# Expert result rows split by the place that makes them: the first half read and added during the last place, and two layer-1 weights queued straight behind the experts'

## The reference, cut to what matters

```python
_, ik = lax.top_k(pe, TOP_K)                      # TOP_K = 2 of 8 in the best of 4 groups
wk = wk / jnp.sum(wk, -1, keepdims=True)
gate = (gmask[:, :, None] * pg_sel[:, None, None] * w_grp[:, None, :]).reshape(-1, N_EXPERTS)
hh = jax.nn.silu(h1) * h3 * gate[:, :, None].astype(t.dtype)
return jnp.einsum('tef,efd->td', hh, p['w2'])     # then x = x + g2 * (this)
```

## Time and profile before

| | |
|---|---|
| median of 3 runs | 978.43 us (975.48 to 981.66) |
| profiled execution: time, span | 978.13 us, 976.3 us |
| mean granted TensorE clock | 0.976 of full speed |
| busy: PE, DVE, ACT, POOL | 896.2, 409.5, 239.9, 120.2 us |
| DMA: bytes, mean rate | 318.85 MB, 327 GB/s |
| places 0 to 31 of layer 0 | about 238 to 468 us |
| seam, to the first projection of tile 0 | 468 to 489 us |
| last matmul to end of layer 1 | 953.1 to 976.3 us |

### The profile page before, as it was taken

One profiled execution on the slowest core, in us unless ns is written; L12 is line 12 of the kernel. 1 busy time (PEld: TensorE's weight loads), 2 busy tenths in 40 slices (PEclk: granted clock), 3 DMA queues, 4 the chain that ended last, 5 costly groups with the idle time before them and its releaser, 6 DMA issues.

```text
span 976.3 us, 14476 instructions
## 1 busy us (share of the span) xinstructions
PE 896.2 (92%) x5479; PEld 503.0 (52%) x5479; DVE 409.5 (42%) x1193; ACT 239.9 (25%) x605; POOL 120.2 (12%) x131
## 2 busy tenths in 40 slices
PE   6999989999999999888999988999989999998880
PEld 3346447556555565455366554554655555645540
DVE  2112476346522442211364576662764225222114
ACT  4020243112111111111354455442211111111111
POOL 1000000100222221211100000001002222212110
PEclk9999999999999999999999999998999999999996
DMA  9999799739999999998870039507599999999975
GB/s 373 397 406 417 292 419 419 247 142 370 364 416 418 402 417 416 418 419 328 330 254 7 1 116 351 234 1 237 212 419 415 417 418 409 417 417 418 412 297 202
DMA packets 62133, 318.85 MB, mean 327 GB/s; under 512 B 12662, under 2 KB 14198, under 8 KB 32104
## 3 DMA queue, kind: packets, MB, share of 16 engines
q1 hardware_dynamic: 46864, 287.51, 72.7%
q0 software_dynamic: 13328, 25.02, 7.4%
q10 hardware_dynamic: 1872, 5.39, 1.5%
HBM read 312.72 MB, written 26.49 MB: 347 GB/s over the span
## 4 chain that ended last, share of the span: by engine, by line
PE 66%; DMA 19%; DVE 9%; issue 2%; ACT 2%; SPq 1%; ACTq 0%; DVEq 0%; POOLq 0%
PE psum L943 15%; DMA ring<-in_l_w 15%; PE psum L956 9%; PE psum L1185 6%; PE psum L1308 3%; PE psum L892 3%; PE psum L879 3%; PE psum L1317 2%; PE psum L923 2%; DMA ring<-in_l_w_ada 2%; PE psum L790 2%; PE psum L1436 2%; PE psum L726 2%; PE psum L1349 2%; PE psum L1411 1%
## 5 line engine op out<-in xcount | busy, mean ns | idle before, releaser
L943 PE MATMUL psum<-ring,scratch 128*64 128x256 f32 x1744 | 210.5, 393 | 22.1 <-DMA ring<-in_l_w 21.1
L943 PEld LDWEIGHTS psum<-ring,scratch 128*64 128x64 f32 x1744 | 135.8, 141 | 81.4 <-issue 32.0
L2350 DVE TENSOR_TENSOR scratch<-scratch,psum 64x256 f32<-64x256 f32 x64 | 27.1, 424 | 286.1 <-ACT scratch L1604 278.9
L956 PE MATMUL psum<-ring,scratch 128*64 128x512 f32 x464 | 112.1, 603 | 1.9 <-ACT scratch L1652 1.0
L2826 POOL DMA_INDIRECT expert_rows<-scratch,slot_rows x64 | 63.5, 992 | 337.5 <-ACT scratch L1618 332.9
L1604 ACT ACTIVATE scratch<-psum 64x256 f32<-64x256 f32 x64 | 24.0, 375 | 255.9 <-PE psum L943 255.9
L1618 ACT COPY scratch<-psum 128x512 f32<-128x512 f32 x64 | 37.5, 585 | 132.1 <-PE psum L956 129.9
L1185 PE MATMUL psum<-ring,scratch 128*128 128x512 f32 (+1 forms) x168 | 63.6, 533 | 0.0
L956 PEld LDWEIGHTS psum<-ring,scratch 128*64 128x64 f32 x464 | 29.3, 136 | 41.5 <-issue 37.3
L1185 PEld LDWEIGHTS psum<-ring,scratch 128*128 128x128 f32 x168 | 31.1, 191 | 29.7 <-issue 28.7
L2332 DVE COPY scratch<-psum 128x512 f32<-128x512 f32 x64 | 41.4, 687 | 7.8 <-PE psum L905 6.9
(11 more groups left out here) (393 smaller groups left out, 1242.3 us busy)
## 6 DMA issues: line engine op xcount, KB each, us to landing
ring<-in_l_w SPq DMA_DIRECT2D x108, 1024.0 KB
ring<-in_l_w_rows SPq DMA_DIRECT2D x56, 1024.0 KB
ring<-in_l_w_ada SPq DMA_DIRECT2D x39, 1024.0 KB, 4.9
ring<-in_ada_first SPq DMA_DIRECT2D x8, 1024.0 KB
ring<-in_l_w_o SPq DMA_DIRECT2D x8, 1024.0 KB
ring<-in_l_w_in SPq DMA_DIRECT2D x4, 1024.0 KB
gate_rows<-gate_rows_hbm POOLq DMA_DIRECT2D x8, 512.0 KB, 7.6
scale_shift<-gate_rows_hbm POOLq DMA_DIRECT2D x8, 512.0 KB, 9.9
```

The source lines that it names most:

```text
L943: last = nc.tensor.matmul(ps[64 * n:64 * n + 64, 2 + par, 0:DE], mine[:, k, :], part(w, k * DE, DE), start=k == 0, stop=k == KD - 1)
L956: last = nc.tensor.matmul(ps[64 * n:64 * n + 64, 5 + par, :], hhT[:, par, k, :], part(w2, k * D + n * 512, 512), start=k == 0, stop=k == 1)
```

## The change

The last expert's rows all go to the second half of the table, so that the first half is complete one place earlier. A token whose first pick is expert 31 has its two picks' rows and gates exchanged (`turned`, `turned_base`, `moved`, `kept`: small DVE operations in the routing). Expert 31 is no longer a candidate for a second turn. For place 31, `down_step(30)` and `take_out(30)` come ahead of the place's own up-projections and silu. SP loads each tile's first rows once places 0 to 30 are stored, and the second rows once place 31 is. DVE adds each half with two operations (gate and g2 in one, then the state); ACT's `scale_pair` is gone. At the seam one `w_in` load and both `w_ukv` loads stand directly behind the experts' weights on SP, and the second stretch of filler on PE has 3 products where it had 8.

The diff, cut to its core:

```diff
@@ tiles of the rows
         def pair(t, k):
-            return view(W, 6144 + (2 * t + k) * D, D) if t < 2 else view(AB, (2 + k) * D, D)
+            if k == 0:
+                return view(W, t * D, D)
+            return view(W, 7168 + 2 * t * D, D) if t < 2 else view(AB, 3 * D, D)
@@ SP
-            def rows_stored(l):
+            def first_rows_stored(l):
                 sp.wait_ge(S[f"ov_out{l}"], 16)
-                for buf in range(2):
-                    sp.wait_ge(S[f"y_out{buf}"], 16 * (l + 1) * PAIRS)
+                sp.wait_ge(S["y_out0"], 16 * (l + 1) * PAIRS)
+                sp.wait_ge(S["y_out1"], 16 * (l + 1) * PAIRS - 16)
...
+            def second_rows_stored(l):
+                sp.wait_ge(S["y_out1"], 16 * (l + 1) * PAIRS)
...
             load_experts(0)
+            load_w_in1(0)
             load(U_UKV, SLOT, A["l1_w_ukv"][0:P, :])
+            load(U_UKV + 1, SLOT, A["l1_w_ukv"][P:2 * P, :])
             sp.wait_ge(S["up_done"], NE)
...
-            load(U_UKV + 1, SLOT, A["l1_w_ukv"][P:2 * P, :])
             load_state(0, 0)
-            rows_stored(0)
-            load_pair(0, 0)
-            load_state(0, 1)
-            load_pair(0, 1)
...
-            load_state(0, 2)
-            load_pair(0, 2)
+            first_rows_stored(0)
+            load_first_rows(0, 0)
+            for t in range(1, NT):
+                load_state(0, t)
+                load_first_rows(0, t)
+            second_rows_stored(0)
+            load_second_rows(0, 0)
+            load_second_rows(0, 1)
+            load_w_in1(1)
+            load_w_in1(2)
+            load_second_rows(0, 2)
@@ PE
                 for e in range(HEAD, NE):
+                    if e == NE - 1:
+                        down_step(e - 1)
                     step(e, pair=e // 2, ahead=e + (4 if e % 2 == 0 else 1) < NE)
-                    if e > HEAD:
+                    if HEAD < e < NE - 1:
                         down_step(e - 1)
...
-            keep_running(8, 2)
+            keep_running(3, 2)
@@ ACT
-            def scale_pair(l, t):
...
-                nc.scalar.activation(pair(t, 0), pair(t, 0), ACT.Identity, scale=gates[:, t, 0:1]).then_inc(S["pair_scaled"], 1)
@@ DVE, before the second place's product
             def route_blocks(l):
+                V.tensor_scalar(row_numbers[:, :, LAST], con[:, C_ROWHI:C_ROWHI + NT], float(RESULT_ROWS), None, ALU.add)
+                V.tensor_copy(turned, pick2[0][:, :, LAST])
@@ DVE
-            def combine(l, t):
...
+            def add_first_rows(l, t):
+                dve.wait_ge(S["g2_in"], 32 * (l + 1))
+                dve.wait_ge(S[f"first_rows{t}"], 16 * (l + 1))
+                link(V.scalar_tensor_tensor(out=pair(t, 0), in0=pair(t, 0), scalar=gates[:, t, 0:1], in1=G[:, cond_of(t), :],
+                                            op0=ALU.mult, op1=ALU.mult))
                 dve.wait_ge(S[f"x{t}_in"], 16 * (l + 2))
+                link(V.tensor_tensor(x[:, t, :], x[:, t, :], pair(t, 0), ALU.add))
+            def add_second_rows(l, t):
...
@@ DVE at the seam
+            add_first_rows(0, 0)
+            add_first_rows(0, 1)
             unit(0)
-            combine(0, 0)
+            add_second_rows(0, 0)
...
             evac_h(2, hT, 1)
-            combine(0, 2)
+            add_first_rows(0, 2)
+            add_second_rows(0, 2)
@@ DVE at the end
             for t in range(NT):
-                combine(1, t)
+                add_first_rows(1, t)
+            for t in range(NT):
+                add_second_rows(1, t)
```

More of the change, by code:

```diff
@@ L621, in load_state, with load_first_rows, load_second_rows @@
                 sp.dma_start(x[:, t, :], X[l][t * P:(t + 1) * P, :]).then_inc(S[f"x{t}_in"], 16)
-            def rows_stored(l):
+            def first_rows_stored(l):
                 sp.wait_ge(S[f"ov_out{l}"], 16)
-                for buf in range(2):
-                    sp.wait_ge(S[f"y_out{buf}"], 16 * (l + 1) * PAIRS)
-            def load_pair(l, t):
-                for k in range(2):
-                    landed = S[f"second_rows{t}" if k and t < 2 else f"pair_rows{t}"]
-                    sp.dma_start(pair(t, k), Y[(k * NT + t) * P:(k * NT + t + 1) * P, :]).then_inc(landed, 16)
+                sp.wait_ge(S["y_out0"], 16 * (l + 1) * PAIRS)
+                sp.wait_ge(S["y_out1"], 16 * (l + 1) * PAIRS - 16)
+            def load_first_rows(l, t):
+                sp.dma_start(pair(t, 0), Y[t * P:(t + 1) * P, :]).then_inc(S[f"first_rows{t}"], 16)
+            def second_rows_stored(l):
+                sp.wait_ge(S["y_out1"], 16 * (l + 1) * PAIRS)
+            def load_second_rows(l, t):
+                sp.dma_start(pair(t, 1), Y[(NT + t) * P:(NT + t + 1) * P, :]).then_inc(S[f"second_rows{t}"], 16)
             def load_first_state(t):
@@ L1632, in experts @@
                 for e in range(4 * LOOPED + 1, NE):
+                    if e == NE - 1:
+                        take_out(e - 1, (e - 1) % 4, (e - 1) // 4)
                     gate(e, e)
-                    if e != HEAD:
+                    if e not in (HEAD, NE - 1):
                         take_out(e - 1, (e - 1) % 4, (e - 1) // 4)
@@ L1884, in _ @@
             experts(1)
-            for t in range(NT):
-                scale_pair(1, t)
             for t in range(NT):
@@ L2322, in route_gates @@
                 link(V.tensor_tensor(wk[:, :, 1], e21, wk[:, :, 0], ALU.mult))
+                moved, kept = blks, mods
+                for k in range(2):
+                    link(V.tensor_tensor(moved[:, k, :], wk[:, :, k], turned, ALU.mult))
+                    link(V.tensor_tensor(kept[:, k, :], wk[:, :, k], moved[:, k, :], ALU.subtract))
+                for k in range(2):
+                    last = V.tensor_tensor(wk[:, :, k], kept[:, k, :], moved[:, 1 - k, :], ALU.add)
+                link(last)
                 link(V.tensor_tensor(gates[:, :, :], wk, over(pg, 2, [P, NT, 2]), ALU.mult))
```

50 lines of the change are left out of this document (25 added, 25 removed).

## The result

The changed kernel takes 984.61 us (median of 5 runs, 982.67 to 989.48) against 978.43 (975.48 to 981.66): ratio 1.0077, 95% interval 1.0048 to 1.0107. It is slower by less than 1%, 5.5 us above the predicted 979.1 and 0.1 us above the upper end of the range. The profiled execution has a span of 984.5 us, 8.2 more than before; that run took 986.31 us, more than the median, so its differences are larger than that of the medians.

The account below looks back on a forecast made before the run. DMA engines are full while experts run; DVE's idle waits for rows at seam and end are on the path. 978.13 plus 0.4 routing, 0.0, 0.7 and 1.7 seam, minus 1.8 end: 979.1 us, range 974.5 to 984.5.

Parts of the forecast that it names:

- Seam, tile 0: 0 us: Seam between layers: tile 0's state ready at 483.85 against 483.91, DVE's old idle time being filled; no loss.
- Shorter filler: +1.7: Seam: with three products PE waits 3.7 us, the clock falls and project1 of tile 0 loses 1.7 us.
- DVE is stuck behind the first rows: Seam rival: tile 1's first rows land 3 us late, delaying unit(0), end without gain; 983.9 us, chance 0.15.
- VectorE's gap: Seam, sign of the slower rival: DVE idle in front of the second pair of first rows (tile 1's).
- Seam, tile 2: +0.7: Seam: DVE does four operations where three were, +1.3 us; about 0.5 us regained at tile 1; +0.7 remains.
- End of layer 1: -1.8: End of layer 1: DVE starts at 956.1 instead of 961.72 and ends at 971.4 instead of 973.19.
- the 7.3 of the row in the prediction: End of layer 1: place 29's rows landed 7.3 us after their put; by it the last tile slips about 1 us.
- the rule on taking turns: DMA engines alternate between queues packet by packet; place 31's rows at layer 1's end then land after 3.2 us.
- Place 30 first: Last places: up-projection of place 31 near 950, second down-projection 0.7 us later, place 30's rows put at 947.7.
- routing: Routing, each layer: two small DVE operations ahead of place 1's product, +0.2 us, ends 0 and 0.4.
- just in time: Seam: first tile in by about 472.6, the second by about 475.5, when DVE asks at 475.9.
- the row of 1.90 us in the prediction: Basis of the filler term: after a 1.90 us wait an up-projection took 5.36 instead of 3.67 us.

Follow-up runs that it names:

- the end alone: Changed kernel with layer 0 and the seam as in the kernel before, only routing and the end of layer 1 changed: 976.58 us, ratio 0.9969.

## Why the prediction was wrong

**The step that failed** is "Seam, tile 0: 0 us", in its last sentence: "The `w_in` load that moved up runs where the share is 0.76, so I cost it nothing". I priced the moved loads by bandwidth and by their effect on the states, and passed over the 16 KB cache piece behind them, for which TensorE waits. It landed after 9.6 us instead of 4.5, and the first rows after 9.7 where I had 3.2. They were in at 476.8, not at 472.6. The runs put 3 to 4 us on the loads. The prediction had named the condition itself, "if the lagging engines got it in front of the states", priced it at 2.4 us and left it out of the sum. A second term was too small: the shorter filler stood at +1.7 and measured 4.3 to 4.6, of which 1.4 to 1.6 lie at the seam.

**The rival that came nearest** is "DVE is stuck behind the first rows", 983.9 at a chance of 0.15. At the seam it is right in size: tile 0's state is ready 20.5 us after the first filler, 15.7 before, so 4.8 later. In mechanism it is half of it, since the expansions held `unit(0)` to within 0.2 us of the same moment. It was wrong that the end would bring nothing. And VectorE's gap stood in front of tile 0's first rows (2.21 us), not in front of tile 1's; that one appears only with the loads back (1.05).

**Shorter filler: +1.7.** Right in mechanism and at the seam, wrong in what it cost over the run. In the profile project1 lost 1.84 us and the transposes ahead of it 0.71. The time lost in runs is 4.3 us in one kernel and 4.6 in the other. The row that I had for it priced one stretch; the mean clock over the run fell by more. In the changed kernel the wait itself is 2.99 us, less than the 3.7 forecast, although tile 0 was later, since the expansions ended later too.

**Seam, tile 2: +0.7.** Measured +0.5: tile 1 to tile 2 takes 11.56 us instead of 11.09, with a wait of 1.48 us for VectorE where the earlier trace rows have 0.68.

**End of layer 1: -1.8.** Right. Counted from the last matmul the profile gives -1.5 and that of the end alone -1.6; in the latter VectorE ends 1.2 us earlier (972.02 and 973.19). The -2.4 counted from the up-projection flatters it, since that starts later with the new order. The time of the end alone is 3.0 us shorter, interval 0.9 to 5.2. Place 31's rows landed after 5.6 us, between the 7.3 of the row in the prediction and the 3.2 that it worked out from the rule on taking turns (the Trainium skill, "DMA: Bandwidth & Descriptors", section "Queues, rings and completion order"); VectorE didn't wait for them.

**Place 30 first, and routing.** Both right in size. With the end alone changed, place 31's up-projection starts at 946.25 and its rows are put at 954.94, where I had 946.3 and 955.2. Routing took +0.14 us (place 0's products to place 2's up-projection), against +0.2. Even with loads and filler as before tile 0 is not at 0: its state is ready 17.5 us after the first filler (483.60 - 466.15), 1.8 later than before, since VectorE waits 1.31 and 1.10 us for the two first tiles, which I had "just in time".

**What stays open.** Layer 1 between seam and end took 4.1 us more in the profile, 3.2 counted between points that the new order leaves alone. The clock is at 0.79 from 708 to 716 us and at 0.72 from 738 to 744, where it was 1.00 at the same times; but at 664 to 680 both kernels have 0.79, and such stretches lie elsewhere in other kernels. That stretch of the program took from 436.3 to 442.0 us over the kernels here, with no one cause found.

## What to carry to other kernels

A load moved forward on a queue is to be priced by the smallest transfer behind it that an engine waits for, not by bandwidth alone. Reading partial results early pays where the engine that uses them is idle and nothing else waits for it (here the kernel's end); elsewhere only what the next consumer needs first may be read early. Before filler is shortened, work out how long TensorE will wait in its place, and measure it: here the shorter filler cost more than twice what the slow products right behind the wait did.

## What the runs showed of the hardware

Waits of TensorE ahead of the same work, and what the work then took: 24 products of tile 0, at full clock 7.05 us, took 7.05 after a wait of 0.75 and of 1.54 us, 8.89 after 2.99, 9.73 after 3.63, 8.70 after 4.03, 8.84 after 5.99 and 9.89 after 7.92 (each also has 1.6 us of waiting between its transposes and itself). The sixteen expansions, 7.11 us at full clock, took 9.78 after 2.73, 9.85 after 2.70, 10.11 after 3.06, and 8.91 after 5.40. A longer wait did not make them slower in proportion.

Nor does the same wait always cost the same. The up-projection of an expert takes 3.67 us at full clock. These two, of the kernel with the end alone and of the kernel before with three products, each had waited 2.46 us:

```profile
458.47 5.36 PE L972 MATMUL psum<-ring,scratch 128*64 128x256 f32 x32 [2.46 <-DMA ring<-in_l_w]
```

```profile
462.48 3.67 PE L943 MATMUL psum<-ring,scratch 128*64 128x256 f32 x32 [2.46 <-DMA ring<-in_l_w]
```

In the thirteen profiles 78 up-projections come behind waits of 1.90 to 3.06 us: 40 of them took 5.19 to 5.36 us, 38 took 3.67. The 59 behind waits of 1.01 to 1.89 us all took 3.67. So the row of 1.90 us in the prediction showed what such a wait can cost and not what it will, and a single slow stretch in a single profile is weak evidence. The products at the seam, slow in all nine cases behind waits of 2.70 us or more, are stronger.

I had not expected that five filler products of 0.88 us each, in a place where TensorE has nothing to do, would be worth 4 us of 978.
